# A two-block transformer layer on one core: squares of the later norms, mixing matmuls and last chunks re-ordered

## The reference, cut to what matters

```python
def rmsnorm(x, w):                       # second_block: rms_norm, the same
    return x * rsqrt(mean(x * x, axis=-1) + EPS) * w
# first_block
    x = x + y @ w_out                                             # stage W1
    x = x + swiglu(rmsnorm(x, ffn_norm_w), w_gate, w_up, w_down)  # F1, D1
# second_block
    proj = rms_norm(x, mix_norm_g) @ w_in                         # VA, UU, Q2, ...
    mixed = einsum('gts,bcsgd->bctgd', tril(w_s), rms_norm(v))    # 4 groups of 192 columns
    x = x + merged @ w_out                                        # W2
    x = x + (gelu(conv3(h2 @ w_up_a)) * (h2 @ w_up_v)) @ w_down   # F2, D2; h2 = rms_norm(x)
return rms_norm(x, final_norm_g)
```

## Time and profile before

| | |
|---|---|
| median of 3 runs | 708.5 us (707.33 to 710.54) |
| profiled execution, its own time | 707.81 us |
| its span, first to last instruction | 706.1 us |
| TensorE busy in the span | 695.9 us |
| mean granted TensorE clock | 0.995 of 2.4 GHz |

### The profile page before, as it was taken

The page is one execution under the profiler, slowest core; times in us unless marked ns, Lnnn a source line. Parts: engine busy times, 40 slices in busy tenths (PEclk is TensorE's granted clock), DMA queues, the critical chain, the costliest instruction groups (busy, mean ns, idle before and its releaser), DMA issues.

```text
span 706.1 us, 12535 instructions
## 1 busy us (share of the span) xinstructions
PE 695.9 (99%) x5312; PEld 658.4 (93%) x5312; DVE 458.3 (65%) x723; ACT 374.8 (53%) x567; POOL 44.0 (6%) x37
## 2 busy tenths in 40 slices
PE   9989999999999999999999999999999999999996
PEld 8869899999999999998988898999999999998885
DVE  5865576876666663545574567558599877887422
ACT  6755764664445544436455565444466666655322
POOL 0320112300000000004000000000030000000000
PEclk9999999999999999999999999999999999999999
DMA  8863134365555565535455424444636555556501
GB/s 307 330 228 117 65 120 152 149 230 188 179 179 187 192 244 197 191 127 216 159 175 198 167 95 163 135 165 178 239 120 220 191 200 197 180 180 239 179 0 59
DMA packets 19959, 124.18 MB, mean 176 GB/s; under 512 B 2240, under 2 KB 3520, under 8 KB 5696
## 3 DMA queue, kind: packets, MB, share of 16 engines
q1 hardware_dynamic: 18000, 120.55, 48.1%
q10 hardware_dynamic: 1904, 2.85, 1.2%
HBM read 122.34 MB, written 1.05 MB: 175 GB/s over the span
## 4 chain that ended last, share of the span: by engine, by line
PE 92%; ACT 2%; DVE 2%; issue 2%; DMA 1%; SPq 1%; POOL 0%; POOLq 0%; ACTq 0%; DVEq 0%
PE pm L307 49%; PE psc L307 32%; PE ptr L307 8%; PE po L307 2%; PE ptr L310 2%; DMA raw<-in_w_dram 1%; ACT wh L316 1%; DVE xl L322 1%; ACT sq L316 1%; DVE wl L319 0%; SPq L397 0%; POOL rcol L319 0%; SPq L336 0%; ACT kvs L313 0%; DVE kvs L319 0%
## 5 line engine op out<-in xcount | busy, mean ns | idle before, releaser
L319 DVE TENSOR_TENSOR wl<-raw,wh 128x1024 fp32r<-128x1024 f32 (+1 forms) x226 | 270.6, 1209 | 55.1 <-ACT wh L316 49.9
L316 ACT ACTIVATE wh<-raw 128x1024 fp32r<-128x1024 f32 (+1 forms) x226 | 229.5, 1036 | 57.3 <-PE psc L307 35.1
L307 PE MATMUL pm<-xh,wh 128*128 128x256 f32 x560 | 159.1, 284 | 0.1
L307 PE MATMUL pm<-xl,wh 128*128 128x256 f32 x560 | 156.4, 279 | 0.0
L307 PE MATMUL pm<-xh,wl 128*128 128x256 f32 x560 | 156.3, 279 | 0.0
L307 PEld LDWEIGHTS pm<-xh,wh 128*128 128x128 f32 x560 | 105.3, 188 | 3.0 <-issue 2.3
L307 PEld LDWEIGHTS pm<-xl,wh 128*128 128x128 f32 x560 | 105.3, 188 | 0.0
L307 PEld LDWEIGHTS pm<-xh,wl 128*128 128x128 f32 x560 | 105.3, 188 | 0.0
L307 PE MATMUL psc<-xh,wh 128*128 128x256 f32 x304 | 85.1, 280 | 0.2 <-DVE xl L322 0.2
L307 PE MATMUL psc<-xl,wh 128*128 128x256 f32 x304 | 84.9, 279 | 0.0
L307 PE MATMUL psc<-xh,wl 128*128 128x256 f32 x304 | 84.9, 279 | 0.0
(11 more groups left out here) (284 smaller groups left out, 1318.3 us busy)
## 6 DMA issues: line engine op xcount, KB each, us to landing
raw<-in_w_dram SPq DMA_DIRECT2D x109, 1024.0 KB, 4.8
early<-in_w_dram SPq DMA_DIRECT2D x2, 1024.0 KB, 12.5
raw<-in_w_dram SPq DMA_DIRECT2D x3, 512.0 KB, 7.3
bias<-in_rel_dram ACTq DMA_DIRECT2D x1, 1024.0 KB, 7.9
xa<-in_xt_dram SPq DMA_DIRECT2D x3, 256.0 KB, 6.5
out_dram<-yo SPq DMA_DIRECT2D x3, 256.0 KB, 2.3
raw<-in_w_dram SPq DMA_DIRECT2D x2, 256.0 KB, 3.7
fgb<-in_fin_dram ACTq DMA_DIRECT2D x1, 512.0 KB, 4.0
```

Of the source, the lines that this page charges most:

```text
L307: return lambda e: e.matmul(dst, lhs, rhs, start=start, stop=stop, skip_group_check=True)
L316: return lambda e: e.activation(dst, src, kind, **kw)
L319: return lambda e: e.tensor_tensor(dst, a, b, op)
```

## The change

Four things are edited. (1) The squares after W1, D1 and W2 are filed in two steps behind the low parts of the last pair, at priority 14 of the slot where the last pair is added, and at priority 16 of the slot after it; VectorE adds them, and it also folds `acc` in `r_sums`. (2) `mix` does both token halves in one step at (UU+2, 60): the matmuls of 128 columns first, then those of 64. (3) `out_last` goes by column halves within a token half. (4) The mean of the final norm: the squares are scaled by 1/32 before squaring, and EPS is added with the sum of the two halves, in one instruction in place of two.

```diff
-        def square_pair(p, ready):
...
+        def square_pairs(p):
+            for q in (p, p + 1):
+                b = q % 2
+                tok["sq", q] = act.do(func(sq[:, b, :], x[:, 2 * q:2 * q + 2, :], ACT.Square), tok["x", q],
+                                      *sq_readers[b])
+                x_readers[q] = [tok["sq", q]]
             if p == 0:
...
+                t = dve.do(tt(acc[:, :], sq[:, 0, :], sq[:, 1, :], ALU.add), tok["sq", 0], tok["sq", 1],
+                           *acc_readers)
+                sq_readers[0], sq_readers[1] = [t], [t]
             else:
...
+                t = tok["acc"]
+                for b in range(2):
+                    t = dve.do(tt(acc[:, :], acc[:, :], sq[:, b, :], ALU.add), tok["sq", p + b], t)
+                    sq_readers[b] = [t]
+            tok["acc"] = t
-        def r_sums(lane=pool):
+        def r_sums(lane=dve):
@@ residual
-                    square_pair(p, [tok["x", p]])
-                    x_readers[p] = [tok["sq", p]]
+            when(ends[3][0], 14, lambda: square_pairs(0))
+            when(ends[3][0] + 1, 16, lambda: square_pairs(2))
@@
+        def mix():
+            after = [tok["wsr"], tok["v2b", "s"]]
+            for bank in S:
+                after += bank.claim()
+            for i in (0, 2, 3, 5):
+                for tb in range(2):
+                    c = (i % 2) * 256 + tb * P
+                    t = pe.do(mm(S[i // 2].ap[:, c:c + P], gv[:, tb, i * P:i * P + P],
+                                 wsr[:, tb, 2 * i // 3, :], True, True), *after)
+                tok["mix", i // 2] = t
+            for i in (1, 4):
+                for tb in range(2):
+                    c = (i % 2) * 256 + tb * P
                     for half in range(2):
+                        h0 = 64 * half
+                        t = pe.do(mm(S[i // 2].ap[h0:h0 + 64, c:c + P], gv[:, tb, i * P + h0:i * P + h0 + 64],
+                                     wsr[:, tb, (2 * i + half) // 3, :], True, True))
+                tok["mix", i // 2] = t
-        when(UU + 2, 60, lambda: mix(0))
-        when(UU + 3, 60, lambda: mix(1))
+        when(UU + 2, 60, mix)
@@ out_last
-                for k in range(FT - TAIL, FT):
-                    out_rows(k, tb)
+                for half in range(2):
+                    for k in range(FT - TAIL, FT):
+                        out_rows(k, tb, (half, ))
@@ out_squares: scale=D_MODEL ** -0.5 is added; out_factor:
-            t = dve.do(tt(m, fss[:, 2 * tb:2 * tb + 1], fss[:, 2 * tb + 1:2 * tb + 2], ALU.add),
+            t = dve.do(stt(m, fss[:, 2 * tb:2 * tb + 1], EPS, fss[:, 2 * tb + 1:2 * tb + 2], ALU.add, ALU.add),
-            t = dve.do(ts(m, m, 1.0 / D_MODEL, EPS, ALU.mult, ALU.add), t)
```

More of the change, by code:

```diff
@@ L586, in build @@
         sq_readers = {0: [], 1: []}
-        def square_pair(p, ready):
-            b = p % 2
-            t = act.do(func(sq[:, b, :], x[:, 2 * p:2 * p + 2, :], ACT.Square), *ready, *sq_readers[b])
-            tok["sq", p] = t
-            if p == 0:
[L594 to L598, removed]
-            else:
-                tok["acc"] = pool.do(tt(acc[:, :], acc[:, :], sq[:, b, :], ALU.add), t, tok["acc"])
-            sq_readers[b] = [tok["acc"]]
+        def square_pairs(p):
[4 more added lines that the diff above has]
+                x_readers[q] = [tok["sq", q]]
+            if p == 0:
+                t = dve.do(tt(acc[:, :], sq[:, 0, :], sq[:, 1, :], ALU.add), tok["sq", 0], tok["sq", 1],
+                           *acc_readers)
+                sq_readers[0], sq_readers[1] = [t], [t]
+            else:
+                t = tok["acc"]
[3 more added lines that the diff above has]
+            tok["acc"] = t
         acc_readers = []
         r_readers = []
-        def r_sums(lane=pool):
+        def r_sums(lane=dve):
             after = O.claim()
@@ L1299, in v_norm @@
                     wsr[:, tb, :, :], wst[:, :, :], rv[:, tb:tb + 1], None, ALU.mult), t, tok["wst"])
[L1301 to L1307, removed]
-                    for half in range(2):
[L1309 to L1320, removed]
+        def mix():
[11 more added lines that the diff above has]
+                    c = (i % 2) * 256 + tb * P
+                    for half in range(2):
+                        h0 = 64 * half
+                        t = pe.do(mm(S[i // 2].ap[h0:h0 + 64, c:c + P], gv[:, tb, i * P + h0:i * P + h0 + 64],
+                                     wsr[:, tb, (2 * i + half) // 3, :], True, True))
+                tok["mix", i // 2] = t
         def u_out(p):
@@ L1335, in gated @@
                 t = dve.do(stt(dst, src, pcol("gg", i), bbc[:, i, :].unsqueeze(1).to_broadcast([P, 2, P]),
-                               ALU.mult, ALU.add), tok["mix", 2 * p + 1], tok["bbc"],
+                               ALU.mult, ALU.add), tok["mix", p], tok["bbc"],
                            *sq_readers[p % 2])
@@ L1609, in out_seed, with out_rows @@
                                                     skip_group_check=True), *after)
-        def out_rows(k, tb):
+        def out_rows(k, tb, halves=(0, 1)):
             s = D2 + k
-            for half in range(2):
+            for half in halves:
                 dst = ob[tb][half].ap
@@ L1645, in out_squares @@
                 tok["osq", tb, half] = act.do(func(sq[:, tb, :], ob[tb][half].ap, ACT.Square,
-                                                   accum_out=fss[:, 2 * tb + half:2 * tb + half + 1]),
+                                                   scale=D_MODEL ** -0.5, accum_out=fss[:, 2 * tb + half:2 * tb + half + 1]),
                                               tok["od", tb, half], *sq_readers[tb])
```

## The result

The changed kernel takes 714.86 us (median of 6 runs, 711.93 to 716.26) where the kernel before takes 707.79 (median of 6 on the same chip, 706.60 to 710.54): a ratio of 1.0102, with an interval of 1.0079 to 1.0125. It is slower, by 7.1 us and not by the 3.25 forecast, and above the top of the range, 714.2. The profiled execution took 714.61 us, 6.80 more than that of before.

What follows compares the result with a forecast made beforehand. TensorE bounds the kernel, busy 695.9 of 706.1 us. W1 and W2 +4.2, VA +0.4, mixing -1.05 and the end -0.3 sum to +3.25 us; against 707.8 that is 711.1, range 706.0 to 714.2.

Steps and rivals of the forecast that it cites:

- The queue of DVE: W1 into F1: the fold, filed behind the low parts, ends at 140.2; TensorE, there at 137.46, waits some 2.7 us.
- each place: Behind W1 and W2: `r_spread` starts 2.1 us later than before, +4.2 us for both.
- The stall for `xl`: At W1 and W2: TensorE's loss of 0.42 us goes once no POOL add runs beside DVE's `xl`.
- the upper bound: W1 and W2: the stretching of DVE isn't POOL's doing and stays; each costs some 5 us, about 717, chance 0.03.
- Mixing: `mix` in one step: 2.99 us in place of 4.04, -1.05 us, bounds 0 and -1.4.
- the end: Last squares and `out_factor`: column halves save 0.10 us, one DVE instruction fewer 0.19; -0.3 us, bounds -0.1 and -0.5.
- The clock falls in the new stall: Rival, F1 and F2: a slower clock follows the 2.7 us wait, 1.7 us lost per fall; 712.8 or 714.5, chance 0.17.
- the likeliest case: Whole kernel: the forecast of 711.1 us, with 709.0 to 713.2 for this case alone, chance 0.66.
- VA: Squares and adds in VA: the fold on DVE ends at 325.4, less up to 0.3; +0.4 us, bounds 0 and +0.8.
- the list of waits: What PEld waits for: one early wait of 3.6 us, which the change doesn't touch, and a few tenths elsewhere.
- the lower bound of (1): W1 and W2: no wait for the squares and every overlap, fold at about 139.5, +1.4 us in each.

Runs made afterwards that it cites:

- e2_fold_pool: The changed kernel with the fold of `acc` back on POOL, squares and adds as changed: 706.23 us, ratio 0.9991 to the kernel before.
- e7_fold_dve: The kernel before with only the fold of `acc` moved from POOL to DVE, squares and adds as they were: 713.82 us, ratio 1.0103.
- e1_fold_early: The changed kernel with the fold on DVE right behind the last two adds, ahead of the low parts: 706.72 us, ratio 0.9981 to the kernel before.
- e6_sums_early: The changed kernel with the fold right behind the last adds, and in F1 and F2 `r_sums` ahead of the last low part: 705.80 us, ratio 0.9973.
- e3_warm: The changed kernel with twelve matmuls on a constant tile added ahead of the sums in F1 and F2: 711.57 us, ratio 1.0048 to the kernel before.
- e8_change_again: The changed kernel once more, unaltered, for a second profile: 716.09 us, ratio 1.0134 to the kernel before.
- e5_fold_18: The changed kernel with the fold in F1 and F2 filed one low part earlier on DVE: 709.42 us, ratio 1.0017 to the kernel before.

## Why the prediction missed

**What held.** The queue of DVE was read rightly, and its sum holds to 0.02 us; that close is luck, since the last 0.16 of it was a guess at overlaps. The prediction's times less the 1.35 us by which this execution reached W1 earlier put TensorE at the sums at 136.11 and the end of the fold at 138.85; the rows say 136.11 and 138.87. With the low clock taken out (3.75 - 1.56) each place costs 2.2 us, for 2.1 predicted. The stall for `xl` is gone and two `xl` take 0.87, so DVE had been stretched by POOL's adds, as the forecast assumed, and the upper bound is out. e2_fold_pool shows the same from the other side: the fold took 1.64 us beside low parts, and they 4.02. The rule cited in the prediction (the Trainium skill, SBUF — State Buffer, "Who interferes with whom") agrees with both. Mixing won 1.04 for 1.05 predicted, the end 0.27 for 0.3. e7_fold_dve shows that the fold alone suffices for a loss of this size, e1_fold_early and e6_sums_early that its place in the queue is the cause and not DVE's added work.

**The step that failed** is the one set down as the rival "The clock falls in the new stall", with a chance of 0.17: "if it is long enough all the same, one fall gives 712.8, two 714.5". It came behind three of the four long waits in the two profiles of the changed kernel, and the mean clocks of its ten runs, 0.987 to 0.996, suggest that it is the usual case. The price was near: 1.7 us for a fall that measured 1.56. Two falls make 3.1 us, and in the forecast's own terms 711.1 + 3.1 = 714.2, against a median of 714.86. What was wrong was to leave the term out of the likeliest case because the new wait is shorter than the one of 3.6 us in the earlier trace rows. The one wait that showed a fall was taken as a lower end, when it only showed that a wait of that size can have one. The prediction also has the length of the idle time decide. The rows don't bear that out: that same wait was 3.7 us in the profiled execution of the change, and the clock held (the last section has the rows). e3_warm settles that the term is real: the same lateness with TensorE kept at work costs 3.3 us (the forecast was 3.25), and without that 3.8 more. The rival that the low clock in the first profile was an accident of one execution falls with it. Why one wait brings a fall and a wait of the same length doesn't stays open. The Trainium skill (TensorE: Matmul & The Clock Gate, "Part 1: The HAM clock gate") has the lower clock as the default state, which activity lifts. That waits are followed by low stretches, and that filling them with matmuls prevents these, agrees with it.

**A smaller miss: VA.** Predicted +0.4 with a bound of 0.8, measured +0.91. The sum there ran from the end of the last `xl` to the end of the fold, 6.37 us; the rows have 6.77 (322.49 to 329.26). The two adds alone are 0.53 longer than assumed, 1.92 for 1.39; overlaps give a little back. The first of them stands beside POOL's select of 1.61 us. No run took the select away, but e7_fold_dve has another pair of the kind: there the fold in VA starts at 325.87, 0.08 us after the select, and takes 0.84 us, twice the 0.42 of the other folds. The rest of the miss is the overlap that I had taken off the sum.

**Two readings of the prediction that don't hold,** though nothing hangs on them: the list of waits has more than one long one and tenths, since TensorE also waits 1.1 us for POOL's `hcp`; and the terms of the lower bound of (1) give a fold at 139.7 and +1.6, not 139.5 and +1.4.

**What the forecast could not hold:** the passes of F1 ran slower in the first execution of the change, 1.06 us over some 180 (183.77 us from 144.18 to 327.95). In e8_change_again the same stretch, 142.05 to 324.76, takes 182.71, as before. So it doesn't belong to the change; nor is it the fall in F1, since behind the fall in F1 of e7_fold_dve the passes stand 116.7 ns apart as before. What it was stays open. It cancels most of the early stretch at a low clock that this execution was spared.

## What to carry to other kernels

Moving a short instruction to another engine, even one that does it faster (0.41 us on DVE, 0.81 on POOL), moves it behind everything filed there: count that queue first, and file the instruction, and what follows it on the chain, ahead of work that isn't due yet. A new wait of the engine that sets the time is priced with the slower clock behind it as a likely case, as soon as the trace shows one such fall anywhere: here 4 of 6 profiled waits of 2.4 to 2.8 us had one. That the wait is shorter than the one that showed it is no reason to leave that out.

## What the runs showed of the hardware that was not expected

Whether the clock falls behind a wait isn't settled by the wait's length here. Behind 2.82 us it fell (the change, F1), behind 2.83 it didn't (e8_change_again, F1); behind 2.4 us it fell in F1 and not in F2 of one execution (e7_fold_dve). The early wait for `kvs`, 3.6 us with a fall behind it before, is as long in the change:

```profile
PEld ptr L310 <- DVE kvs L319: 3.7, 1, 3.7
```

But there the window behind it is at full clock:

```profile
40.00:44.00 4.00, 4.00 (x23) 3.32 (x22) 4.00 (x5) 1.92 (x3) 0.00 (x0) 1.00 0.49 205
```

Each fall seen behind a wait for `acc` was a stretch of some 3.4 us at 0.50 of the clock. e1_fold_early, which has no wait for `acc`, shows such a stretch all the same, at 86.7, though TensorE is shown busy for 3.64 of the 3.70 us before it; its window:

```profile
86.70:90.10 3.40, 3.40 (x17) 3.40 (x17) 2.43 (x3) 3.32 (x6) 0.00 (x0) 0.50 0.20 27
```

Executions of one kernel spread by several us with the clock they were granted, 707.06 us at 0.999 to 711.92 at 0.991 in e5_fold_18. So one profile isn't enough to say whether a wait brings a fall. The mean granted clock of all the runs says how much low clock there is, and a run with the wait filled, as e3_warm, what it costs.
